# Short convolution of q, k and v as diagonal products on TensorE, and one root and one reciprocal for eight head norms

## What is computed

```python
D_MODEL = 1024; SEQ = 512; CONV_WIDTH = 4; N_GDN_HEADS = 4; GDN_HEAD_DIM = 128

def l2norm(x):
    return x * lax.rsqrt(jnp.sum(x * x, axis=-1, keepdims=True) + EPS)

def gdn_mixer(qkv, z, a_gate, b_gate, conv_w, a_log, dt_bias, gdn_norm_g):
    qkv = jax.nn.silu(causal_depthwise_conv(qkv, conv_w)).astype(f32)
    q, k, v = jnp.split(qkv, 3, axis=-1)
    q = l2norm(heads(q)) * (GDN_HEAD_DIM ** -0.5)
    k = l2norm(heads(k))
    v = heads(v)
    ...
    o = gated_delta_rule(q, k, v, g, beta).transpose(0, 2, 1, 3)

def s5_mixer(u, ...):                       # runs beside it in the kernel
    bu = lax.complex(einsum(b_bar.real, ug), einsum(b_bar.imag, ug))
    _, states = lax.associative_scan(_linear_recurrence_combine, (a, bu), axis=1)
    y = einsum(c_c, states).real
    y = gelu(y + d_skip * u)

def hybrid_mixer(h, w_in, ...):
    proj = h @ w_in                         # u_s5 (512) | qkv (1536) | z (512) | gates (8)
    ...
    return jnp.concatenate([y_s5, y_gdn], axis=-1) @ w_out
```

## Time and profile before

| | |
|---|---|
| median of 3 runs | 3214.39 us (3213.19 to 3214.4) |
| the profiled execution: its own time | 3215.19 us |
| its span in the trace | 3213.4 us |
| busy: PE, DVE, ACT, POOL | 2880.9 (90%), 1178.4 (37%), 618.6 (19%), 322.3 (10%) us |
| mean granted PE clock | 0.932 of full speed (2.4 GHz) |
| DMA | 312.05 MB, mean 97 GB/s |

### The profile page before, as it was taken

One profiled execution on the slowest core, in us unless ns is written; L12 is line 12 of the kernel. 1 busy time (PEld: TensorE's weight loads), 2 busy tenths in 40 slices (PEclk: granted clock), 3 DMA queues, 4 the chain that ended last, 5 costly groups with the idle time before them and its releaser, 6 DMA issues.

```text
span 3213.4 us, 36202 instructions
## 1 busy us (share of the span) xinstructions
PE 2880.9 (90%) x14067; PEld 2113.0 (66%) x14067; DVE 1178.4 (37%) x2162; ACT 618.6 (19%) x1268; POOL 322.3 (10%) x344
## 2 busy tenths in 40 slices
PE   7877786967996899999999999999987799999998
PEld 3322276432332787687888888888865587888787
DVE  4799864220113441703333202123435603333202
ACT  1002222010111362711111101111125401111100
POOL 1344130011220000000000000000015400000000
PEclk8888898978998999899999999999969999999999
DMA  6222100449983112011221122121200011221122
GB/s 245 79 79 79 79 14 9 188 174 370 375 359 150 40 66 79 1 53 53 79 79 65 65 105 105 66 79 65 78 27 1 1 53 53 79 79 65 66 105 79
DMA packets 49442, 312.05 MB, mean 97 GB/s; under 512 B 12192, under 2 KB 14496, under 8 KB 18336
## 3 DMA queue, kind: packets, MB, share of 16 engines
q1 hardware_dynamic: 39520, 290.28, 24.0%
q0 software_dynamic: 9216, 17.85, 1.5%
q10 hardware_dynamic: 576, 2.10, 0.2%
HBM read 351.08 MB, written 16.78 MB: 114 GB/s over the span
## 4 chain that ended last, share of the span: by engine, by line
PE 63%; DVE 3%; issue 1%; ACT 1%; DVEq 1%; POOLq 0%; POOL 0%; ACTq 0%
PE ps L480 34%; PE ps L923 17%; PE ps L966 2%; PE ps L888 1%; DVE u L1551 1%; PE ps L1090 1%; PE ps L906 1%; PE ps L1062 1%; PE ps L874 1%; PE ps L1085 1%; PE ps L913 1%; PE ps L1117 0%; PE ps L819 0%; PE ps L1088 0%; PE ps L1040 0%
## 5 line engine op out<-in xcount | busy, mean ns | idle before, releaser
L480 PE MATMUL ps<-u,ring 128*128 128x264 f32 (+1 forms) x5248 | 1251.2, 401 | 8.6 <-DVE u L1554 5.2
L480 PEld LDWEIGHTS ps<-u,ring 128*128 128x128 f32 x5248 | 1000.9, 191 | 264.8 <-issue 103.0
L923 PE MATMUL ps<-work,ring 128*128 128x264 f32 x2432 | 557.1, 389 | 10.8 <-DVE work L1551 8.9
L923 PEld LDWEIGHTS ps<-work,ring 128*128 128x128 f32 x2432 | 466.1, 192 | 93.3 <-DVE work L1551 9.7
L1548 DVE TENSOR_SCALAR work<-tmp,par 128x528 f32<-128x528 f32 (+2 forms) x140 | 86.6, 618 | 662.5 <-ACT tmp L1451 335.6
L1554 DVE SCALAR_TENSOR_TENSOR work<-tmp,par,work 128x528 f32<-128x528 f32 (+2 forms) x332 | 273.6, 824 | 50.9 <-issue 46.4
L1551 DVE TENSOR_TENSOR work<-work 128x512 f32<-128x512 f32 (+8 forms) x335 | 187.2, 600 | 61.8 <-ACT work L1323 18.4
L2120 DVE RECIPROCAL rs<-rs 128x264 f32<-128x264 f32 x8 | 14.4, 1803 | 529.5 <-ACT rs L1393 528.4
L751 PE MATMUL ps<-work,u 128*64 128x512 f32 x640 | 175.3, 614 | 27.8 <-DMA work<-in_experts,rs 25.6
L1451 ACT ACTIVATE tmp<-ps 128x528 f32<-128x528 f32 x80 | 48.9, 612 | 499.7 <-PE ps L480 499.7
L2365 POOL TENSOR_TENSOR work<-u,work 128x256 f32<-128x256 f32 (+1 forms) x40 | 24.5, 612 | 1090.3 <-DVE u L1551 1090.3
(11 more groups left out here) (332 smaller groups left out, 2876.3 us busy)
## 6 DMA issues: line engine op xcount, KB each, us to landing
ring<-in_stream SPq DMA_DIRECT2D x169, 1024.0 KB, 4.8
work<-in_experts SPq DMA_DIRECT2D x25, 2048.0 KB, 17.1
work<-in_experts SPq DMA_DIRECT2D x25, 1024.0 KB, 7.9
ring<-in_experts SPq DMA_DIRECT2D x7, 2048.0 KB, 13.2
ring<-in_experts SPq DMA_DIRECT2D x7, 1024.0 KB, 9.3
work<-rows_out SPq DMA_DIRECT2D x4, 1024.0 KB, 7.9
h<-in_x_fm SPq DMA_DIRECT2D x1, 2048.0 KB, 10.5
rows_in<-work ACTq DMA_DIRECT2D x4, 512.0 KB, 2.6
```

The source lines that it names most:

```text
L480: m = pe.matmul(pair(q, half, cnt), ring[:, (n + b // 16) % WSLOTS, b % 16 * P:(b % 16 + 1) * P], x[:, lo:lo + cnt], start=(k == 0), stop= ...
L923: return pe.matmul(pair(q0 + t, half, HALF), block(t, kk), rhs[kk][:, half * HALF:(half + 1) * HALF], start=(kk == 0), stop=(kk == parts - 1))
```

## The change

The four taps of the convolution become four matmuls that accumulate in PSUM. ACT writes four diagonal 128x128 matrices for a tile (`conv_taps`, identity times the tap's column), PE multiplies them with `cbuf` shifted by 0 to 3 columns (`conv_out`) into the bank from which the tile itself had been copied, and ACT applies SiLU from PSUM and, for q and k, squares the result (`conv_silu`). DVE's convolution goes away. The bank is released (`tile_read`) by the SiLU and no longer by the copy.

The sums of squares of the eight heads are written as eight rows of one 8x512 result (`l2_sum`, with a stationary matrix of eight columns of which one is ones) in steps 2 to 9. One root on 8 partitions (ACT, end of step 10) and one reciprocal on 8 partitions (DVE, end of step 10) replace eight of each on 128. A matmul with a selecting 8x128 matrix spreads a row over the 128 partitions (`l2_spread`, two a step in steps 11 to 14), and DVE multiplies with it straight from PSUM (`head_normed`, two a step, one before and one after the S5 work).

```diff
@@ -250,6 +250,8 @@
         s5s = at(30040, 24, S5_TILES)
         sig = p5[0]
         cbuf = [tmp[:, b, 0:SEQ + 3] for b in range(2)]
+        taps = [at(1024 + CONV_C * P * b, CONV_C, P) for b in range(2)]
+        l2r = rs[0:8, 0:SEQ]
         wgate = at(WORK - 64, DT, 8)
 
         beta, gate, csum, gtot, ecs, etail, egt, bcs, sp1, sp2, sp3, sp4 = [
@@ -559,19 +561,39 @@
                                   start=(n == 0), stop=(n == 1), tile_position=(0, lo))
                 m.then_inc(sem("s5_out_done"), 1)
 
+            def conv_out(i):
+                pe.wait_ge(sem("conv_in"), i + 1)
+                for t in range(CONV_C):
+                    m = pe.matmul(pair(q0 + NS5 + i), taps[i % 2][:, t, :], cbuf[i % 2][:, t:t + SEQ],
+                                  start=(t == 0), stop=(t == CONV_C - 1))
+                m.then_inc(sem("conv_done"), 1)
+
+            def l2_sum(i):
+                pe.wait_ge(sem("squares_ready"), DT + i + 1)
+                pe.matmul(ps[0:8, 1, 0:SEQ], ccol("pick", 7 - i, 8), sq[:, i % 2, 0:SEQ], start=(i == 0), stop=(i == 7)
+                          ).then_inc(sem("squares_used"), 1)
+
+            def l2_spread(i):
+                pe.wait_ge(sem("l2_ready"), 1)
+                if i:
+                    pe.wait_ge(sem("qk_ready"), i)
+                pe.matmul(ps[:, 1, 0:SEQ], ident[0:8, i:i + 1].broadcast_to([8, P]), l2r, start=True, stop=True
+                          ).then_inc(sem("l2_spread"), 1)
+
             for j in range(S5_TILES):
                 in1(NS5 + j)
+                if 1 <= j < 13:
+                    conv_out(j - 1)
+                if 11 <= j < 15:
+                    l2_spread(2 * (j - 11))
                 s5_in(j)
                 if j == 0:
                     pe.wait_ge(sem("mod_read"), 1)
                 mod_unit(MOD2_UNIT[j], 2 * j, 32, 3)
-                if j >= 8:
-
-                    pe.wait_ge(sem("squares_ready"), j + 1)
-                    if j > 8:
-                        pe.wait_ge(sem("l2_read"), j - 8)
-                    pe.matmul(ps[:, 1, 0:SEQ], ones, sq[:, j % 2, 0:SEQ], start=True, stop=True
-                              ).then_inc(sem("squares_used"), 1)
+                if 2 <= j < 10:
+                    l2_sum(j - 2)
+                if 11 <= j < 15:
+                    l2_spread(2 * (j - 11) + 1)
                 if j:
                     s5_out(j - 1)
             s5_out(S5_TILES - 1)
@@ -587,7 +609,7 @@
             pe.matmul(ps[:, 3, 448:464], upto, gate, start=True, stop=True)
             pe.matmul(ps[:, 3, 480:496], ones, gate, start=True, stop=True).then_inc(sem("csum_done"), 1)
             pe.wait_ge(sem("qk_ready"), 8)
-            pe.wait_ge(sem("silu_qkv"), 12)
+            pe.wait_ge(sem("tile_read"), Q0["in1"] + NS5 + 14)
             pe.wait_ge(sem("csum_read"), 1)
             for c in range(CHUNKS):
                 tok = slice(c * P, (c + 1) * P)
@@ -1158,41 +1180,44 @@
 
             act.wait_ge(sem("mod_done"), 8)
             act.activation(modrow, ps[:, 3, 0:P], ACT.Copy).then_inc(sem("mod_copied"), 1)
-            def head_root(i):
-                act.wait_ge(sem("squares_used"), DT + i + 1)
-                if i:
-                    act.wait_ge(sem("qk_ready"), i)
-                else:
-                    act.wait_ge(sem("norm_applied"), 1)
-                act.activation(rs[:, 0:SEQ], ps[:, 1, 0:SEQ], ACT.Sqrt, bias=eps).then_inc(sem("l2_read"), 1)
-
+            def conv_taps(i):
+                if i >= 2:
+                    act.wait_ge(sem("conv_done"), i - 1)
+                for t in range(CONV_C):
+                    act.activation(taps[i % 2][:, t, :], ident, ACT.Copy, scale=pcol("conv_w", 12 * t + i))
+
+            def conv_silu(i):
+                act.wait_ge(sem("conv_done"), i + 1)
+                act.activation(qkv[:, i, :], pair(q0 + NS5 + i), ACT.Silu).then_inc(sem("tile_read"), 1)
+                if i < 8:
+                    act.wait_ge(sem("squares_used"), DT + i - 1)
+                    act.wait_ge(sem("tile_read"), q0 + NS5 + i + 3)
+                    act.activation(sq[:, i % 2, 0:SEQ], qkv[:, i, :], ACT.Square).then_inc(sem("squares_ready"), 1)
 
             q0 = Q0["in1"]
+            conv_taps(0)
+            conv_taps(1)
             for t in range(NS5):
                 act.wait_ge(sem("tile_done"), q0 + t + 1)
                 act.activation(us5[:, t, :], pair(q0 + t), ACT.Copy).then_inc(sem("tile_read"), 1)
+            act.wait_ge(sem("pads_ready"), 1)
             for j in range(16):
                 q = q0 + NS5 + j
                 act.wait_ge(sem("tile_done"), q + 1)
                 if j < 12:
                     if j >= 2:
                         act.wait_ge(sem("conv_done"), j - 1)
-                    else:
-                        act.wait_ge(sem("pads_ready"), 1)
-                    act.activation(cbuf[j % 2][:, 3:], pair(q), ACT.Copy).then_inc(sem("tile_read"), 1)
-                else:
+                    act.activation(cbuf[j % 2][:, 3:], pair(q), ACT.Copy).then_inc(sem("conv_in"), 1)
+                if 1 <= j < 13:
+                    conv_silu(j - 1)
+                    if j + 1 < 12:
+                        conv_taps(j + 1)
+                if j >= 12:
                     act.activation(z1[:, j - 12, :], pair(q), ACT.Silu).then_inc(sem("tile_read"), 1)
-                if 1 <= j < 13:
-                    act.wait_ge(sem("conv_done"), j)
-                    act.activation(qkv[:, j - 1, :], qkv[:, j - 1, :], ACT.Silu).then_inc(sem("silu_qkv"), 1)
-                if j >= 8:
-
-                    act.wait_ge(sem("silu_qkv"), j - 7)
-                    act.wait_ge(sem("squares_used"), j - 1)
-                    act.activation(sq[:, j % 2, 0:SEQ], qkv[:, j - 8, :], ACT.Square).then_inc(sem("squares_ready"), 1)
-                    if j > 8:
-                        head_root(j - 9)
-            head_root(7)
+                if j == 10:
+                    act.wait_ge(sem("squares_used"), DT + 8)
+                    act.wait_ge(sem("norm_applied"), 1)
+                    act.activation(l2r, ps[0:8, 1, 0:SEQ], ACT.Sqrt, bias=eps[0:8, :]).then_inc(sem("l2_read"), 1)
             act.wait_ge(sem("mod_done"), 24)
             act.activation(modrow, ps[:, 3, 0:P], ACT.Copy).then_inc(sem("mod_copied"), 1)
 
@@ -1702,19 +1727,15 @@
             dve.drain().then_inc(sem("s5_angle"), 1)
             def head_normed(i):
 
-                dve.wait_ge(sem("l2_read"), i + 1)
-                dve.reciprocal(rs[:, 0:SEQ], rs[:, 0:SEQ])
-                dve.drain()
-                stt(qkv[:, i, :], qkv[:, i, :], float(P) ** -0.5 if i < HEADS else 1.0, rs[:, 0:SEQ], mul, mul
+                dve.wait_ge(sem("l2_spread"), i + 1)
+                stt(qkv[:, i, :], qkv[:, i, :], float(P) ** -0.5 if i < HEADS else 1.0, ps[:, 1, 0:SEQ], mul, mul
                     ).then_inc(sem("qk_ready"), 1)
 
 
             q0 = Q0["in1"]
             for j in range(S5_TILES):
-                if j < 12:
-                    dve.wait_ge(sem("tile_read"), q0 + NS5 + j + 3)
-                    conv(qkv[:, j, :], cbuf[j % 2], CONV_C, lambda t: pcol("conv_w", 12 * t + j), None, SEQ
-                         ).then_inc(sem("conv_done"), 1)
+                if 11 <= j < 15:
+                    head_normed(2 * (j - 11))
                 dve.wait_ge(sem("table_ready"), j + 1)
                 dve.wait_ge(sem("s5_in_done"), j + 1)
                 C, Sn = table[j % 2]
@@ -1743,14 +1764,16 @@
                     dve.wait_ge(sem("s5_out_done"), j - 1)
                 tt(st5[j % 2][0], p5[0], p5[1], sub)
                 tt(st5[j % 2][1], p5[2], p5[3], add).then_inc(sem("s5_state_ready"), 1)
-                if j >= 9:
-                    head_normed(j - 9)
+                if j == 10:
+                    dve.wait_ge(sem("l2_read"), 1)
+                    dve.reciprocal(l2r, l2r).then_inc(sem("l2_ready"), 1)
+                if 11 <= j < 15:
+                    head_normed(2 * (j - 11) + 1)
                 if j >= 4 and j % 4 == 0:
                     t = j // 4 - 1
                     dve.wait_ge(sem("s5_out_done"), 4 * t + 4)
                     stt(y5[:, t, :], us5[:, t, :], pcol("s5_d", t), ps[:, 6 + t % 2, 0:SEQ], mul, add
                         ).then_inc(sem("y5_ready"), 1)
-            head_normed(7)
             dve.wait_ge(sem("s5_out_done"), S5_TILES)
             stt(y5[:, 3, :], us5[:, 3, :], pcol("s5_d", 3), ps[:, 7, 0:SEQ], mul, add).then_inc(sem("y5_ready"), 1)
             dve.wait_ge(sem("mod_turned"), 2)
```

## The result

The changed kernel takes 3172.12 us in the median (3169.22 to 3177.16), the kernel before, timed beside it, 3213.79. The ratio is 0.9872, with a 95% interval of 0.9858 to 0.9885: 41.7 us faster. A later timing of the same program gave 3179.3 (3169.08 to 3179.66) against 3214.85, ratio 0.9875, interval 0.9852 to 0.9897. So the direction and the size in per cent repeat, and the microseconds of the whole program don't to better than some 7. The forecast was 3183, 3173 to 3200.

A forecast was written before the change was run, and what follows sets the result against it. DVE bounds the kernel at 18.1 us a step and PE would become the bound at 15.45 to 16.47. A gain of 35.6 us less 4.3 for the clock, 31.3, takes 3215.19 to 3183.9, median 3183; range 3173 to 3200.

The forecast's parts named there:

- What bounds the kernel: Loop: DVE full at 18.1 us a step; after the change PE bounds at 15.45, or 16.47 with a head sum.
- The sum: Step times added from tile 1 to the GLU product: gain 35.6 us, 31.3 after the clock allowance, giving 3183.9 us.
- 4.3 for the clock: Steps 11, 13 and 14: half of the possible 0 to 8.7 us lost if the clock falls behind the waits.
- two other rules of the Trainium skill: PE cycling through PSUM banks loses its clock; a DVE operation with two SBUF inputs and a POOL operation lock each other out.
- The period without a sum: PE's step without head sum: tile 7.06, convolution 3.63, S5 inputs 1.91, narrow unit 1.01, state product 1.84, in all 15.45 us.
- 6.3 of waits: Three PE waits of 2.1 us each at the first spread in steps 11, 13 and 14.
- the 8.7 that I gave as the most: After three waits, spread and S5 inputs each take 2.9 us more if the clock falls: 0 to 8.7 in all.
- ACT and DMA at nothing: Per step: ACT's 3 us of 16 hide under PE's work and DMA gains no load, so neither costs time.
- Rival 1: Clock oscillates in the new loop: 15 steps lose 1.75 us each, 26 us, giving 3206; chance 0.09.
- Rival 2: POOL hinders S5 more: DVE at 15.1 us a step, showing at the reciprocal and steps 12 to 14; 3192; chance 0.10.
- The y5 write that I named as a sign: DVE's y5 write, with one PSUM input, takes 0.74 us, taken as agreeing that PSUM inputs escape POOL's lockout.
- Rival 3: Slower: 5.8 us of narrow products a step lose the clock into the next tile; 3235 at 7.5 us; chance 0.05.

The follow-up runs named there:

- the runs with one engine's work increased: Changed kernel with PE's four convolution products done twice: 3206.3 us; changed kernel with two more PSUM products on DVE per S5 step: loop 256.46 us.
- The sum apart: Changed kernel with the head sum between the tile and the convolution product instead of ahead of the state product; 3178.74 us, loop 260.15.
- the sum on partitions 32 to 39: Changed kernel with the eight sums, root, reciprocal and spreads on partitions 32 to 39 instead of 0 to 7; loop 251.10 us in one execution.
- the early reciprocal: Changed kernel with the root and reciprocal at the end of step 9 instead of step 10; 3162.87 us, ratio 0.983.
- the second head in the middle: The early reciprocal kernel with DVE multiplying the second head of steps 11 to 14 mid-step instead of at its end; 3166.22 us, ratio 0.9848.
- the convolution twice: Changed kernel with the four convolution products done twice into the same bank; 3206.3 us in one execution, loop 288.22.

## Why the prediction was right or wrong

*What bounds the kernel* was right: DVE set the pace, PE became the bound in steps 1 to 10 with mostly 3 to 4 us of idle DVE, as the runs with one engine's work increased show.

*The sum* was 8.0 us too long in the loop (260.6 forecast, 252.57 measured). By its own terms:

| us | forecast | first trace of the change | second trace |
|---|---|---|---|
| steps 1 to 10 | 162.7 | 152.96 | 152.96 |
| steps 11 to 14, with 4.3 for the clock | 73.3 | 74.75 | 75.51 |
| step 15 to the GLU product | 24.6 | 24.86 | 25.76 |

- The step that failed is to add up the groups of PE one behind the other: the term is the head sum at 1.02 us in each of steps 2 to 9. I took it from the row at 337.60, where it is a product with 128 columns. The new one has 8. Six of eight cost nothing, two cost 0.85: 1.7 us instead of 8.2. The sum apart and the sum on partitions 32 to 39 show the cause.
- The Trainium skill bears on this, in "TensorE: Matmul & The Clock Gate", section "The mechanism" of the part on packing small matmuls: each 32x32 tile of the array can hold weights of its own and compute an output slice of its own, so that tiles at different positions overlap. The traces agree, with starts 0.01 to 0.02 us apart, down to which partitions collide. I had weighed two other rules of the Trainium skill and not this one, though the diff has `ps[0:8, ...]` next to a product that writes `ps[lo:lo + 32, ...]`.
- The period without a sum was forecast at 15.45 and is 15.12, 3.3 us over ten steps. The convolution is 3.52 (3.63 forecast), the tile 6.97 (7.06), the narrow unit 0.90 (1.01). I had charged each group the same 0.19 beyond 0.43 a record; the tile and the convolution behind it cost 0.09 and 0.08.
- Steps 11 to 14 came out nearly right by luck, by errors that cancel. Forecast were 62.7 us of products, 6.3 of waits and 4.3 for the clock. At full clock and without waits the four steps take 59.2 (16.31, 17.17, 12.87 and 12.87 in the traces of the early reciprocal and the second head in the middle). The waits were 4.2, and what is left of 74.75 is 11.3 for the clock. The products are 3.5 shorter, mostly because the first spread ran beside the S5 inputs in steps 11, 13 and 14 and cost nothing, some 1.0 us each. That is the same failed step.
- The waits of 2.25 and 1.94 came at steps 11 and 14. That of step 13 didn't: the clock fell in step 12 without a wait and cost PE 3.2 us, more than the 1.94 that it waits in step 13 where the clock stays (the trace of the early reciprocal).
- The clock's 11.3 us are above the 8.7 that I gave as the most. I had the half clock end with the S5 inputs; in step 11 it lasted through the narrow unit, the second spread and the state product into the next tile (7.54), 4.5 us. Step 12's fall, 3.2 us and 0.5 in the tile behind it, wasn't in the sum at all.
- ACT and DMA at nothing: right. No row shows PE waiting for a SiLU or for taps. The reciprocal on 8 partitions takes 3.33 us, as long as that on 128.

*Rival 1* (the clock oscillates): not in steps 1 to 10, where the granted clock is 1.00 over 151 us, with two uses of a bank in every step. The rule of the Trainium skill that the prediction names ("TensorE: Matmul & The Clock Gate", "A second HAM failure mode: psum-queue depth-cycling") speaks of a PE that idles briefly between groups. PE was busy for 151.00 of these 151.00 us, so that condition was not met and the rule is not tested here.

*Rival 2* (POOL hinders S5 more): no. S5 stays at 11.98 us; only in step 1 two sums took 1.86 instead of 1.29. The y5 write that I named as a sign (388.53) was a poor row, since POOL stands idle there. Those at 183.64 and 255.88 of the same trace, beside POOL's operations at 183.31 and 255.55, take 0.73, so the reading itself holds.

*Rival 3* (narrow work loses the clock): something of its kind came, at one place and far smaller. In step 12 the clock fell in a row of narrow products without a wait, in both traces of the change and in three more (the sum apart, the convolution twice, the second head in the middle), and cost 3.7 us in the first. That the narrow products are the cause is not shown, as the same row kept the clock in two traces.

*The range.* The low end of 3173 allowed 5 us for cheaper groups and a shorter reciprocal on top of the clock. The cheaper groups came to 9.7 in steps 1 to 10 and to some 3.5 more behind them, while the reciprocal wasn't shorter and the clock cost 11.3. The measured 3172.12 lies 0.9 below the range and the second timing, 3179.3, inside it; the stages behind the loop scatter by more than the 0.9. The loop's 8 us are not scatter.

*What stays open* is what decides between the fall of step 12 and none. The same PE code kept the clock with tile 12 at 266.59 and lost it with tile 12 at 263.06, so the code of the step alone doesn't decide. No run here tried it by itself, and the cause stays open.

## What to carry to other kernels

Before adding up the groups of TensorE, note for each product which groups of 32 input partitions (rows of the array) and of 32 output partitions (columns) it uses. Here two neighbours with different output groups, or with different input groups, cost no more than the longer of the two. So a narrow sum is best placed beside a narrow product with other output partitions, and its cost is not that of a full-width one. When a bound moves from one engine to another, look for small serial steps of the old bound (here one reciprocal) that can move to where that engine now idles: one step earlier was worth 6.8 us in its own step, because a 2.25 us wait also cost 4.5 us of clock. Judge effects below 10 us of a 3200 us program inside the trace, and the total only over several runs.

## What the runs showed of the hardware that was not expected

- A product with a stationary matrix of 128x8 and one of 128x32 ran at the same time although both used all 128 rows: starts 0.01 to 0.02 us apart when the output partitions lay in different groups of 32, one after the other (0.86 us apart) when they lay in the same. Products with inputs of 8 and of 32 partitions did the same when these lay in different groups of 32 (260.78 and 260.79 us with the early reciprocal), though both wrote all 128 partitions.
- TensorE's clock fell to 1.2 GHz in a step without a recorded stop, during a row of products with 8 rows, 32 rows or 32 columns (273.56 to 283.31 us), and stayed at 2.4 GHz through the same row of products in another kernel (277.09 to 283.76 us). It fell in four of the six traces with this row.
- A reciprocal of 8x512 takes 3.33 us on DVE, that of 128x512 3.34.
